# Loading expert matrices in long pieces: neighbouring rows in one partition, with token columns and hidden units permuted to match

## The reference

```python
scores = sigmoid(h @ router_w)                  # (tokens, 16)
# the best of 4 groups of experts, then the best two experts in it; their scores are scaled to sum to 1
for e in range(N_EXPERTS):                      # 16
    a = silu(h @ w1[e]) * (h @ w3[e])           # w1, w3: (1024, 512)
    out = out + gates[..., e:e + 1] * (a @ w2[e])   # w2: (512, 1024)
```

## Time and profile before

| what | value |
|---|---|
| median of 3 runs | 1459.95 us (1452.65 to 1463.16) |
| span of the profiled execution (first to last instruction) | 1453.6 us |
| median of the runs less that span | 6.3 us |
| TensorE busy | 1190.9 us, 82% of the span |
| experts of layer 0 in the span | about 464 to 763 us |
| experts of layer 1 in the span | about 1136 to 1426 us |
| bytes moved | 336.33 MB, of which queue q1 (SP) 286.36 MB |

### The profile page before, as it was taken

The page is one execution under the profiler, slowest core; times in us unless marked ns, Lnnn a source line. Parts: engine busy times, 40 slices in busy tenths (PEclk is TensorE's granted clock), DMA queues, the critical chain, the costliest instruction groups (busy, mean ns, idle before and its releaser), DMA issues.

```text
span 1453.6 us, 14992 instructions
## 1 busy us (share of the span) xinstructions
PE 1190.9 (82%) x5437; PEld 646.6 (44%) x5438; DVE 470.4 (32%) x1036; ACT 267.9 (18%) x506; POOL 153.9 (11%) x189
## 2 busy tenths in 40 slices
PE   3999899798975999999870899989766687779892
PEld 1454455444433545545430444456543443434441
DVE  1443666555015111111114483243433311111112
ACT  2231211655013000100103221110012100100001
POOL 0030111000110011100106200000001110101102
PEclk8899899999997999999996899975569798989996
DMA  9584156792032899999996822220004599999983
GB/s 335 184 315 145 62 179 232 265 387 96 0 115 87 293 392 372 389 377 325 381 380 255 275 91 82 84 91 0 1 0 145 205 376 380 378 390 379 390 314 109
DMA packets 143083, 336.33 MB, mean 231 GB/s; under 512 B 7723, under 2 KB 9907, under 8 KB 143019
## 3 DMA queue, kind: packets, MB, share of 16 engines
q1 hardware_dynamic: 128619, 286.36, 54.4%
q0 software_dynamic: 13536, 45.95, 9.0%
q10 hardware_dynamic: 864, 3.15, 0.5%
HBM read 303.39 MB, written 32.05 MB: 231 GB/s over the span
## 4 chain that ended last, share of the span: by engine, by line
PE 66%; DMA 16%; DVE 9%; ACT 3%; issue 3%; SPq 2%; POOL 1%; POOLq 0%; DVEq 0%
DMA ring<-in_moe_w 13%; PE psum L1754 10%; PE psum L1122 7%; PE psum L1751 6%; PE psum L1031 6%; PE psum L514 5%; PE psum L1781 4%; PE psum L1776 3%; PE psum L506 3%; PE psum L1135 2%; PE psum L350 2%; PE psum L1718 2%; PE psum L1361 2%; PE psum L1362 2%; PE psum L487 1%
## 5 line engine op out<-in xcount | busy, mean ns | idle before, releaser
L1751 PE MATMUL psum<-ring,arena 128*64 128x256 f32 x1408 | 167.7, 396 | 31.4 <-DMA ring<-in_moe_w 17.9
L1751 PEld LDWEIGHTS psum<-ring,arena 128*64 128x64 f32 x1408 | 116.9, 142 | 77.6 <-DMA ring<-in_moe_w 20.6
L1754 PE MATMUL psum<-ring,arena 128*128 128x512 f32 x320 | 143.2, 607 | 5.8 <-ACT arena L1823 4.2
L1862 DVE TENSOR_TENSOR arena<-arena,psum 128x512 f32<-128x512 f32 x32 | 22.0, 688 | 319.3 <-issue 220.1
L1776 PE MATMUL psum<-ring,arena 128*64 128x512 f32 x352 | 90.7, 662 | 28.6 <-DMA ring<-in_moe_w 28.6
L1122 PE MATMUL psum<-arena,ring 128*128 128x512 f32 (+1 forms) x256 | 97.8, 540 | 0.0
L1754 PEld LDWEIGHTS psum<-ring,arena 128*128 128x128 f32 x320 | 61.3, 194 | 82.0 <-issue 76.0
L1031 PE MATMUL psum<-ring,arena 128*128 128x512 f32 x192 | 82.9, 593 | 1.5 <-ACT arena L1016 1.5
L1829 ACT ACTIVATE arena<-psum 128x512 f32<-128x512 f32 x32 | 19.1, 598 | 335.3 <-PE psum L1776 223.4
L1854 DVE COPY arena<-psum 128x512 f32<-128x512 f32 x32 | 22.1, 692 | 171.0 <-PE psum L1776 102.4
L1781 PE MATMUL psum<-ring,arena 128*128 128x512 f32 x160 | 72.7, 609 | 3.7 <-DMA ring<-in_moe_w 2.7
(11 more groups left out here) (365 smaller groups left out, 1544.8 us busy)
## 6 DMA issues: line engine op xcount, KB each, us to landing
ring<-in_moe_w SPq DMA_DIRECT2D x96, 2048.0 KB, 15.8
ring<-in_w_mod SPq DMA_DIRECT2D x24, 2048.0 KB, 9.0
ydram<-arena POOLq DMA_DIRECT2D x32, 512.0 KB, 13.3
ring<-in_od_w_in SPq DMA_DIRECT2D x6, 2048.0 KB, 10.4
ring<-in_ev_w_in SPq DMA_DIRECT2D x3, 2048.0 KB, 12.8
ydram<-arena POOLq DMA_DIRECT2D x44, 128.0 KB, 5.4
ydram<-arena POOLq DMA_DIRECT2D x20, 256.0 KB, 6.7
ring<-in_ev_w_out SPq DMA_DIRECT2D x2, 2048.0 KB, 12.2
```

What stands on the lines that cost most here:

```text
L1751: mm = pe.matmul(psum[64 * g:64 * g + 64, j, 0:256], xT[b][:, k, 0:64], w[:, k, 256 * g:256 * g + 256], start=k == 0, stop=k == KD - 1)
L1754: mm = pe.matmul(bank(j), xT[b][:, k, :], w[:, k, :], start=k == 0, stop=k == KD - 1)
```

## The change

Three things are edited, and they belong together.

1. `expert_src` gives partition p neighbouring rows. For w1 and w3 these are the eight rows 8p to 8p+7, one piece of 16 KB; for w2 two neighbouring rows out of each half of 256, two pieces of 8 KB. The bytes, the slots and the number of DMAs stay.
2. The router's copy out of PSUM permutes the 1024 token columns, so that block k of a gathered and transposed token is feature 8p+k. The one copy of 1024 columns per tile becomes two of 512, which read PSUM with a step of eight floats and write runs of 16 floats.
3. VectorE's product of silu and h3 permutes the hidden units in each half of 256 into the even ones and then the odd ones. It is still one instruction of 512 columns; it reads with a step of two floats.

```diff
     def expert_src(l, kind, e):
...
-        return we.rearrange("(k p) n -> p k n", p=P)
+        if kind == "w2":
+            return we.rearrange("(g p k) n -> p g (k n)", p=P, k=2)
+        return we.rearrange("(p k) n -> p (k n)", p=P).unsqueeze(1)
...
+    def expert_rows(v):
+
+        return v.rearrange("p (r k j) -> p r k j", r=KD, k=KD)
+
     def act_router(l, tiles):
...
             act.wait_ge(*act_more("back_full"))
-            act.activation(htok[:, t, :].rearrange("p (b n) -> p b n", b=2), psum[:, 2 * (i % 2):2 * (i % 2) + 2, :], ACT.Copy
-                           ).then_inc(S("back_act"), 1)
+            for half in range(2):
+                last = act.activation(expert_rows(htok[:, t, :])[:, :, 4 * half:4 * half + 4, :],
+                                      bank(2 * (i % 2) + half).rearrange("p (k j r) -> p r k j", k=4, r=KD), ACT.Copy)
+            last.then_inc(S("back_act"), 1)
...
+    def ah_blocks(v):
+        return v.rearrange("p (g k q) -> p g k q", g=2, k=2)
+
+    def hidden_blocks(v):
+
+        return v.rearrange("p (g q k) -> p g k q", g=2, k=2)
+
     def dve_moe(l):
...
-            dve.tensor_tensor(ah[b], sil[b], bank(1), ALU.mult).then_inc(S("a_done"), 1)
+            dve.tensor_tensor(ah_blocks(ah[b]), hidden_blocks(sil[b]), hidden_blocks(bank(1)), ALU.mult).then_inc(S("a_done"), 1)
```

More of the change, by code:

```diff
@@ L2077, in body @@
             dve.wait_ge(extra(l, "sil"), n + 1)
-            dve.tensor_tensor(ah[0], sil[0], bank(1), ALU.mult).then_inc(extra(l, "a"), 1)
+            dve.tensor_tensor(ah_blocks(ah[0]), hidden_blocks(sil[0]), hidden_blocks(bank(1)), ALU.mult).then_inc(extra(l, "a"), 1)
             dve.wait_ge(extra(l, "at"), n + 1)
```

## The result

The changed kernel is slightly slower: 1464.69 us in the median (20 runs) against 1457.94 us for the kernel before (20 runs), ratio 1.0062 with a 95% interval of 1.0041 to 1.0083. The two medians differ by 6.8 us; the means of the same runs differ by 8.9 us, which is what the ratio amounts to. The change is within 1%, as forecast, but its sign is the other one: 11.4 us less were forecast. The time lies inside the wide range (1432 to 1478 us), which takes in most of the rivals, and outside the forecast's own range of 1440 to 1457 us. The profiled execution has a span of 1459.7 us, against 1453.6 us.

The account below looks back on a forecast made before the run. DMA engines were taken to bound 330 us of the experts, TensorE the other 220. Terms -14, -4.9, +7 and +0.5 gave -11.4 us: span 1442.2, median 1448.5 us; own range 1440 to 1457, wide range 1432 to 1478.

Parts of the forecast that it names:

- the rate: Expert loads: 8 KB pieces would move at 423 GB/s and 16 KB pieces at 430, against 387 and 410.
- nothing gained: Lower bound on faster expert loads: long pieces could meet a limit at the memory, so loads get no shorter.
- no higher rate: Rival: 16 KB pieces stay at 387 to 400 GB/s, gathers still cost 7 us; +3 us, 1463 us; chance 0.13.
- layer 1: Expert loads of layer 1: ceiling 17.5 us, of which four fifths, 14 us, were counted as gained.
- inside the slack: Layer 1's gathers: nearly all narrow, they land 2 us later without making anything wait.
- late gathers in layer 0, +7 us: Layer 0's experts: TensorE waits 8.7 us for later gathers, counted as 7; bounds 0 and some 50 us.
- the ring fills: Layer 0: loads run on while TensorE waits for gathers, sparing later load waits; lowers 8.7 us to 7.
- faster loads in layer 0: Last 70 us of layer 0's experts: 12 loads bound by DMA get shorter, 4.9 us gained.
- the rest at +0.5: Router's copies split in two and read in steps: 0.5 us slower in all, bounds 0 and 4.7; VectorE's product 0.
- The upper bound for the copy: Router's copy reading PSUM in steps of eight floats might take twice as long, costing up to 4.7 us.
- Finely mixed queues: Rival: engines mix the two queues finely, gathers stay at 7 us; about -20 us, 1440 us; chance 0.25.
- The slow rival: Two long pieces before every gather or store piece; full store and gather 13 us later; about +40, 1500 us; chance 0.17.

Follow-up runs that it names:

- early16: The changed kernel with its 16 and 8 KB pieces, each gather issued one expert earlier; ratio to the kernel before 0.9907.
- q8: The changed kernel with all expert load pieces 8 KB, rows taken from the two halves of each matrix; ratio to the kernel before 0.9932.
- early_before: The kernel before, pieces of 2 and 4 KB, with each gather issued one expert earlier; ratio to the kernel before 0.9994.
- strided: The kernel before with its loads, but router copies and VectorE's product reading and writing in strides, values in place; ratio to the kernel before 0.9996.
- small16: The changed kernel with each store cut to 16 rows, one execution; the gather at about 507 us landed after 13.8 us instead of 15.7.
- p2: The changed kernel with loads written as 2 KB (w1, w3) and 4 KB (w2) pieces, but moved as before the cut; ratio to the kernel before 1.0093.
- p4: The changed kernel with loads written as 4 KB pieces, but still moved as 16 and 8 KB; ratio to the kernel before 1.0068.
- p8: The changed kernel with loads written as 8 KB pieces, but still moved as 16 and 8 KB; ratio to the kernel before 1.0096.
- q4: The changed kernel with 4 KB pieces, w1 and w3 rows from four quarters, w2 and VectorE's product as before; ratio to the kernel before 0.9916.
- fullg16: The changed kernel with every gather fetching 128 rows, one execution; median landing in layer 1 10.5 us instead of 9.4.

## Why the prediction was wrong, point by point

**Right: the rate.** 8 KB and 16 KB pieces were put at 423 and 430 GB/s; windows with them alone show 428 and 428 (430 in early16, at 1172.5 to 1176.5 us). In the DMA records of layer 0's experts a piece of 8 KB takes 309 ns (q8) and one of 16 KB 611 ns (changed) in the median, where 310 and 610 were computed. The bound "nothing gained" and its rival, no higher rate, fell.

**Right in kind, mis-sized: layer 1.** 14 us were counted, 7.9 were measured; the 44 loads were issued in 242.7 us (1160.7 to 1403.4), where 238 were forecast and 252 was the time before. The loads alone are not the cause: with the gathers early on both sides, long pieces take 12.3 us off layer 1's experts (289.4 in early_before, 277.1 in early16). What is missing is what I took to be inside the slack. TensorE in layer 1 of the changed kernel:

```profile
PE psum L1784 <- DMA ring<-in_moe_w: 18.4, 8, 3.1
PE psum L1726 <- DMA arena<-hdram,idxg: 8.1, 3, 5.4
```

Before it had no wait for a gather in the loop there. Narrow gathers did land 2 us later, as predicted (7.2 to 9.4 us), but faster loads also shorten the expert and with it the time that a gather has.

**Wrong, and the step that failed: "late gathers in layer 0, +7 us".** The mechanism was named, and the two places shown were nearly right: 5 us for the first (15.73 instead of 10.11, 5.6 later) and 2.7 for the second, where TensorE waited 2.0. Three things were wrong.
- "The other gathers of layer 0 stand at the median, with 5 us of slack and more." The landings do not rise evenly: those issued at 605.9 and 724.6 us landed after 13.4 and 10.9 us and held TensorE too, and the one at 689.2 after 15.2 us, for a wait of 3.5 us where I had counted 1. Together 15.9 us in five waits instead of 8.7 in three. And part of the slack was time in which TensorE waited for loads. The gather of 724.6 us is an example: before, it was issued at 705.3 us and landed 8.4 us ahead of its use, but TensorE waited 3.6 us for a load in between; in the changed kernel that wait is gone, and TensorE stands 2.6 us for the gather.
- "While TensorE stands, the ring fills, which spares a part of later load waits." Four slots are soon full. Then the DMA engines stand as well, which is the share of 0.88 for 0.97 above. Load waits did shrink, from 15.7 to 3.5 us, but from the expert at 674.3 us (687.0 after) to the end of the layer it takes 88.4 us before and 88.2 after: what the loads gained there, the gathers took. The 4.9 us of faster loads in layer 0 did not show.
- A cost that stood in no step: TensorE's clock after a wait. The chain at the first late gather, and the clock around it (wait, then the 5 us after it; the third column from the end is the granted clock):

```profile
502.06 15.73 DMA arena<-hdram,idxg
517.83 1.98 PE psum L1726 x8
```

```profile
511.20:517.80 6.60, 0.00 (x0) 0.00 (x0) 0.69 (x1) 0.60 (x1) 2.13 (x3) 0.75 1.00 418
517.80:523.00 5.20, 4.62 (x13) 3.17 (x14) 1.29 (x2) 0.60 (x1) 0.00 (x0) 0.50 1.02 430
```

After 6.6 us of nothing the clock is at 0.50 (1.2 GHz of 2.4) for the next 5 us, and eight transposes take 1.98 us instead of 1.11. Four more groups behind waits are slow: the product at 583.2 us takes 15.44 us instead of 13.97, the 64 half-width matmuls at 707.9 and 738.3 us 9.35 and 9.51 instead of 7.13, and those at 763.9 us 5.22 instead of 3.65. The kernel before has such places as well, but fewer. This is its product behind the gather of 502.75 us, 1.7 us longer than the others:

```profile
514.98 15.67 PE L1754 MATMUL psum<-ring,arena 128*128 128x512 f32 x32 [0.62 <-DVE arena L1848]
```

Two groups at 712.0 and 746.4 us, behind waits for loads, are its others (5.36 us instead of 3.67 each). So only the difference counts, and it can be read from the experts of layer 0 as a whole, before and after; the first number behind the length is the time that TensorE was busy:

```profile
464.40:762.80 298.40, 273.12 (x1239) 143.97 (x1240) 42.73 (x64) 29.95 (x50) 31.71 (x48) 0.97 0.97 355
463.70:775.20 311.50, 279.66 (x1239) 147.47 (x1239) 42.99 (x64) 30.00 (x49) 31.80 (x48) 0.94 0.90 342
```

The same 1239 matmuls keep TensorE busy 6.5 us longer, at a clock of 0.94 for 0.97. That is one half of the 13.1 us. The other half, 6.6 us, is idle time: 14.9 us more for gathers, 12.2 us less for loads, and some 4 us of waits put down to "issue". early16, with the same loads, has the 0.97 again: it is the late gathers that bring the low clock.

Forecast against result, then: layer 0 at +2.1 us (7 for gathers, 4.9 off for loads) came to +13.1, layer 1 at -14 came to -7.9, and the rest at +0.5 came to +0.9; -11.4 became +6.1 us in the profiled executions. Layer 0 alone missed by 11 of the 17.5 us. That the result is "within 1%" all the same is luck: the forecast put it there by a gain of 11.4 us, and it came there because a gain of 7.9 us and a loss of 13.1 us nearly cancel.

**Right, and worth nothing: the copies.** The router's copies take 594 ns each, in the slack as before; VectorE's product takes 688 ns as before. The upper bound for the copy did not apply to this form, and applied in strided, where it writes with a step as well. The Trainium skill ("SBUF — State Buffer", section "Door 1: The DMA port swizzle") says that PSUM works in lines of 8 bytes and non-contiguous access slows matmuls much; for ScalarE's copy the trace shows nothing of it, 594 ns with a step of eight floats against 597 without. The same section's line of 16 bytes for SBUF fits the 1112 ns of the copy that writes every eighth float.

**The rivals.** Finely mixed queues (no late gathers) is out: landings rose by 2.4 us in the median, and the longest by 5.6. The rival without a higher rate had the nearest time, 1463 us, and the wrong reason: the rate rose to 428 GB/s. The slow rival, two long pieces before each piece of q0 with 13 us more for a full store and gather, is out by size; the truth lies between it and the forecast. On the rule from "DMA: Bandwidth & Descriptors", section "Queues, rings and completion order" of the Trainium skill, a queue at a time, packet by packet: that landings grow with the length of the load pieces (7.1, 7.5, 9.1, 9.5 us) and with the gather's own pieces agrees with it; small16 and the packets counted beside it show that a count of turns does not give the size.

## What to carry to other kernels

Before making the pieces of a bulk transfer longer, look for small transfers that share the engines and for the slack of whoever waits for them. Here 4 or 8 KB pieces took nearly all the rate that could be had, and 16 KB turned the gain into a loss, until the gathers were issued one expert earlier. A buffer that is free an expert before it is used is cover that cost nothing here (early_before, 0.9994); take it before, not after, raising the load on a shared resource. And do not count a wait of TensorE as the wait alone: the matmuls behind it may run at half the clock, which here was half of what layer 0 lost.

## What the runs showed of the hardware that was not expected

- Neighbouring rows that are contiguous on both sides are moved as one piece, whatever the access pattern says: 63083 records in p2, p4, p8 and the changed kernel alike. A test of piece length must keep the pieces apart in memory.
- 8 KB pieces move at 428 GB/s, as fast as 16 KB pieces (428 to 430); 4 KB pieces at 410 (in q4 too, from 1210 to 1214 us), 2 KB at 387.
- A ScalarE copy of 512 floats from PSUM with a read step of eight floats and written runs of 64 takes 594 ns, like a plain one; written with a step of eight it takes 1112 ns.
- Late gathers and a low TensorE clock go together. Over layer 0's experts the mean granted clock is 0.92 to 0.94 in the profiled executions of the five kernels with 16 KB pieces, full stores and no early gather (changed, p2, p4, p8, fullg16), and 0.97 to 0.99 in the eleven others.
- A landing of up to 14.8 us need not cost anything: in early16 no transposes in the loop wait for a gather.
